# The six products of a panel step ordered by token half instead of by product

## The reference

```python
qa, ka, va, qb, kb, vb, gates = split_proj(rmsnorm(xp, g_norm1[l]), w_in[l])
oa = swa_prompt(qa, ka, va, rel_bias_table, swa_sinks[l])     # sliding-window attention
ob = sb_prompt(qb, kb, vb)                                    # stick-breaking attention
xp = merge_ffn(xp, oa, ob, gates, w_proj_a[l], w_proj_b[l], w_out[l], g_norm2[l], w_up[l], w_down[l])
...
def merge_ffn(x, oa, ob, gates, w_proj_a, w_proj_b, w_out, g_norm2, w_up, w_down):
    g = jax.nn.sigmoid(gates.astype(jnp.float32)).astype(x.dtype)
    merged = g[..., :D_MODEL] * (oa @ w_proj_a) + g[..., D_MODEL:] * (ob @ w_proj_b)
    x = x + merged @ w_out
    u = jnp.square(jax.nn.relu(rmsnorm(x, g_norm2) @ w_up))
    return x + u @ w_down
```

## Time and profile before

| | |
|---|---|
| Time, median of 3 runs | 832.81 us (832.44 to 832.97) |
| Profiled execution, its own time | 832.35 us |
| Its span in the profile | 830.5 us |
| PE busy | 818.9 us, 99% of the span, 6205 matmuls |
| PEld busy | 802.6 us, 97% of the span, 6205 weight loads |
| DVE, ACT, POOL busy | 624.1, 391.5, 294.9 us |
| Granted TensorE clock | 0.998 of full speed |
| DMA | 78.18 MB, mean 94 GB/s |

### The profile page before, as it was taken

How to read it: one execution, slowest core, us unless ns; L and a number is a source line. 1 busy time by engine, 2 the same in 40 slices (tenths; PEclk the granted TensorE clock), 3 DMA queues, 4 the chain that set the end, 5 groups by cost and what they waited for, 6 DMA issues and landing times.

```text
span 830.5 us, 16017 instructions
## 1 busy us (share of the span) xinstructions
PE 818.9 (99%) x6205; PEld 802.6 (97%) x6205; DVE 624.1 (75%) x1075; ACT 391.5 (47%) x668; POOL 294.9 (36%) x213
## 2 busy tenths in 40 slices
PE   9999999999999999999999999999999999999996
PEld 7999999999999989999999999999999999999995
DVE  5587876356889999876338888488965889488996
ACT  5657775244667757653332333233433243333532
POOL 2562222225545544254444200642025400552330
PEclk9999999999999999999999999999999999999999
DMA  8743112451112211143313113422134213422203
GB/s 279 257 148 100 52 51 65 152 166 52 52 52 82 70 51 51 51 165 127 102 53 102 52 52 102 152 70 83 51 101 128 74 51 101 132 70 66 85 2 115
DMA packets 68449, 78.18 MB, mean 94 GB/s; under 512 B 2552, under 2 KB 65072, under 8 KB 68016
## 3 DMA queue, kind: packets, MB, share of 16 engines
q1 hardware_dynamic: 68080, 76.92, 28.8%
q10 hardware_dynamic: 320, 0.60, 0.2%
HBM read 70.15 MB, written 8.93 MB: 95 GB/s over the span
## 4 chain that ended last, share of the span: by engine, by line
PE 87%; DVE 9%; issue 2%; ACT 1%; DMA 1%; ACTq 0%; DVEq 0%
PE pan L1567 56%; PE pan L1783 12%; PE att L1783 11%; PE att L1721 1%; PE att L1694 1%; PE pan L1623 1%; DVE sp_lo L1161 1%; PE att L1711 1%; PE att L1567 1%; DVE sp_hi L1159 1%; DVE xT L1400 1%; PE att L1863 1%; DMA grow<-in_g 1%; PE pan L1656 1%; DVE ob_lo L1223 1%
## 5 line engine op out<-in xcount | busy, mean ns | idle before, releaser
L475 POOL TENSOR_TENSOR w_lo<-raw,w_hi 128x512 fp32r<-128x512 f32 x160 | 222.0, 1413 | 422.0 <-ACT w_hi L817 180.0
L1567 PE MATMUL pan<-a_hi,w_hi 128*128 128x288 f32 x624 | 133.7, 295 | 0.0
L1567 PE MATMUL pan<-a_lo,w_hi 128*128 128x288 f32 x624 | 133.4, 295 | 0.0
L1567 PE MATMUL pan<-a_hi,w_lo 128*128 128x288 f32 x624 | 132.9, 295 | 0.0
L1567 PE MATMUL pan<-h_hi,w_hi 128*128 128x288 f32 x512 | 109.6, 295 | 0.0
L1567 PE MATMUL pan<-h_lo,w_hi 128*128 128x288 f32 x512 | 109.4, 295 | 0.0
L1567 PE MATMUL pan<-h_hi,w_lo 128*128 128x288 f32 x512 | 109.0, 295 | 0.0
L1567 PEld LDWEIGHTS pan<-a_hi,w_hi 128*128 128x128 f32 x624 | 99.7, 188 | 1.0
L1567 PEld LDWEIGHTS pan<-a_hi,w_lo 128*128 128x128 f32 x624 | 100.0, 188 | 0.0
L1567 PEld LDWEIGHTS pan<-a_lo,w_hi 128*128 128x128 f32 x624 | 99.5, 188 | 0.0
L1783 PE MATMUL pan<-F_hi,w_hi 128*128 128x288 f32 x320 | 95.7, 299 | 0.6 <-DVE xT L1400 0.6
(11 more groups left out here) (283 smaller groups left out, 1766.8 us busy)
## 6 DMA issues: line engine op xcount, KB each, us to landing
raw<-in_w_in SPq DMA_DIRECT2D x34, 512.0 KB, 4.9
raw<-in_w_up SPq DMA_DIRECT2D x32, 512.0 KB, 4.8
raw<-in_w_down SPq DMA_DIRECT2D x32, 512.0 KB, 4.8
raw<-in_w_out SPq DMA_DIRECT2D x8, 512.0 KB, 4.1
x_spill<-xT SPq DMA_DIRECT2D x1, 2304.0 KB, 7.0
xT<-x_spill SPq DMA_DIRECT2D x1, 2304.0 KB, 11.0
x_rows<-in_x_prompt SPq DMA_DIRECT2D x4, 512.0 KB, 6.7
raw<-in_w_pa SPq DMA_DIRECT2D x4, 512.0 KB, 4.6
```

Source lines behind the costliest of these rows:

```text
L475: last = nc.gpsimd.tensor_tensor(w_lo[:, slot, k:k + 4, :], raw[:, rs, k:k + 4, j * P:(j + 1) * P], w_hi[:, slot, k:k + 4, :].bitcast(F32) ...
L1567: got = nc.tensor.matmul(out[:, h, 0:HALF], w, x[:, h * HALF:(h + 1) * HALF], start=first and n == 0, stop=last and n == 2)
```

## The change

In `mm3` the two loops are exchanged. Before, each of the three products is issued for the first half of tokens and then for the second. Now the three products of the first half come first, then the three of the second. Flags (`start` with the first product, `stop` with the last) stay with their product, so each PSUM bank still gets its three terms in the same order. No offset of a buffer, no wait and no other engine's instruction is touched.

```diff
             def mm3(out, wh, wl, xh, xl, first, last):
 
-                for n, (w, x) in enumerate(((wh, xh), (wh, xl), (wl, xh))):
-                    for h in range(2):
+                for h in range(2):
+                    for n, (w, x) in enumerate(((wh, xh), (wh, xl), (wl, xh))):
                         got = nc.tensor.matmul(out[:, h, 0:HALF], w, x[:, h * HALF:(h + 1) * HALF],
                                                start=first and n == 0, stop=last and n == 2)
                 return got
```

## The result

The change makes the kernel slower by a quarter of a per cent: 834.94 us at the median of 17 runs against 832.81 us at the median of 17 of before, a ratio of 1.0023 with a 95% interval of 1.0016 to 1.0030. One run after the change, 992.03 us at a granted clock of 0.752, counts in the median and not in the ratio; without it the median is 834.82 us. The forecast was 838.2 us, in a range of 829.4 to 841.5: the direction was right and the time inside the range, but of the 5.4 us of loss that were forecast only 2.1 came.

The account below looks back on a forecast made before the run. The prediction took TensorE's distance between matmul starts as the bound: 3,840 panel matmuls moving to 133.3 ns add 5.4 us, everything else 0, so 832.8 + 5.4 = 838.2 us, in a range of 829.4 to 841.5 us.

Parts of the forecast that it names:

- What bounds the kernel: TensorE, busy 818.9 of 830.5 us: time is its number of matmuls times the distance between their starts.
- So one bank three times in a row has no price of its own: Panels: three successive matmuls to one PSUM bank cost nothing, since products do that and reach 131.1 ns.
- I take the high rung as the panels' new one: +5.4 us: All 3,840 panel matmuls go to 133.3 ns between starts, 512.0 us against 506.6; chance 0.42.
- the middle one: Distance of 132.2 ns between matmul starts, 793.3 ns per six; seen in panels in the old order.
- the low rung: Distance of 131.1 ns between matmul starts, 786.7 ns per six; seen in panels and products before the change.
- A change between high and low parts moves the read address by 32 bytes against a grid of 64: Panel steps: such changes take the time; the new order has two from high to low and two back, before one each.
- The direction: Sign of the whole change: slower with chance 0.59, same 0.19, faster 0.22.
- The ladder: Six matmuls of a step take 786.7, 793.3 or 800 ns, 6.7 ns apart; any other time would disprove the reason.
- The rival "by turns": Panels take both of the products' distances, 131.1 and 133.3 ns, by turns: +1.1 us (-0.3 to +2.5); chance 0.25.
- The dearer rung: Panels: both changes from high to low cost the dear one's time, 135.0 ns: +8.7 to +11.8 us; chance 0.14.
- All on the low rung: All panel matmuls at 131.1 ns: -3.1 us, with the first chunk's products -3.7 us; chance 0.19.
- The products' own shift: Down projection's products may take another distance from the phase the panels leave: 0 taken, -0.6 to +1.2 us allowed.

Follow-up runs that it names:

- e3: Changed kernel with the output bank alternating from matmul to matmul, reads in the new order; 834.41 us, ratio 1.0024 to the kernel before.
- e16: Kernel before (old order) with high parts of `a` and `h` at residue 64, low parts at 32 modulo 256; 834.85 us, ratio 1.0020.
- e1: Changed kernel (new order) with the activations' low parts at the same residue as the high parts, 64 modulo 256; 833.53 us, ratio 1.0014 to before.
- e2: Kernel before (old order) with the activations' low parts at the same residue as the high parts; 833.88 us, ratio 1.0013.
- e13: Changed kernel (new order) with low parts of `a` and `h` at residue 32 modulo 256, high parts kept at 64; 830.58 us, ratio 0.9974 to before.
- The snake: Third order at present offsets: first half high, low; second half low, high; then low weights with second half, first half; 835.11 us, ratio 1.0030 to before.
- e8: The kernel before, run again without any change; 832.18 us.
- e12: Changed kernel (new order) with high parts at residue 0 and low parts at 32 modulo 256; 835.50 us, ratio 1.0036 to before.
- e17: e13 with `ob_lo` and the products' `F_hi` and `F_lo` at residues 64 and 32 too, new order; 829.74 us, ratio 0.9952 to before.
- e9: New order with `a` and `h` at residues high 0, low 224 modulo 256, and `a` moved 256 bytes later; 833.53 us, ratio 1.0010 to before.
- e10: New order with `a` and `h` at residues high 0, low 224, and the second area holding `h` 256 bytes later; 833.66 us, ratio 1.0011 to before.

## Why the prediction was right in direction and wrong in size

**What bounds the kernel: right.** The loss is in the distance between starts of panel matmuls (0.56 ns x 3,840 = 2.15 us, against 2.13 us between the medians), and nothing is left over for another place. Waits stayed, loads stayed at 6205, and the groups' busy time rose to 151 us as computed.

**"So one bank three times in a row has no price of its own": right,** and shown by e3, where the banks alternate and the times stay.

**"I take the high rung as the panels' new one: +5.4 us": the step that failed.** It rested on "no panel is on the high rung in the old order and no product on the middle one, so the rungs on offer seem to go with the order". They go with the pair of order and addresses. The two were never seen apart in the trace of before, since each order had its own residues. e16 has the old order on the high rung, and the changed kernel itself has the new order on the middle one. The term of the sum that was mis-sized is thus the panels' new rung: put at 133.3 ns for all 3,840, it measured 132.2 and 133.0 ns by stretches, 132.49 on average, and +2.15 us in place of +5.4. The caution in the same paragraph, that the products' addresses aren't the panels', was the true point, and it should have cost the high rung its lead: with it gone, the products said nothing on the panels beyond a spread of 131 to 133.3 ns. I used it against the low rung alone.

**"A change between high and low parts moves the read address by 32 bytes against a grid of 64": half right.** The shift is needed for the order to matter at the present place of the high part: without it e1 and e2 are alike at 132.2 ns. The grid of 64 was an assumption that no row showed, and residues modulo 64 don't name the rungs: e13 has the same ones as the changed kernel and another distance. But counting the changes doesn't give the price. The snake with two a step has 132.8 ns, dearer than the 132.49 ns on average of the new order with four, and the new order at 64 and 32 has all four and the lowest rung of all.

**The direction: in part luck.** At 64 and 32, with as many changes by 32 bytes as at 64 and 96, the same exchange of loops gains 3.8 us (e13, e16). No reason in the prediction tells these two cases apart, so it couldn't have known the sign for this kernel's offsets.

**The ladder: incomplete.** I took the distances as the step's 786.7, 793.3 or 800 ns. A pattern may repeat over several steps, and it is its whole length that falls on the ladder: in the changed kernel 2,393.3 ns for three steps (359 x 6.67), in the snake 1,593.3 ns for two (239 x 6.67). So 133.0 and 132.8 ns are rungs too. The prediction had called its reason wrong if a step took a time off its ladder, and the single steps of 799 and 801 ns do. The step of 6.7 ns held; the row of six matmuls to which I applied it did not.

**The rival "by turns"** had a price of -0.3 to +2.5 us, into which the 2.1 us fall, but for another pair of rungs than it named. What it had right is that stretches draw among rungs, which e8 shows. **The dearer rung** fell at these addresses: 133.0 ns was the dearest, though e12 shows that offsets can bring more. **All on the low rung** was off for this change and came true one edit further, in e17, with a price near the one given (-3.1 us there; -4.0 us in e17, 0.0048 x 832.81). Of that the panels have only 2.5 us, by their mean of 131.27 ns; the products have most of the rest.

**The products' own shift:** -0.6 to +1.2 us was allowed. The first chunk's went down to 131.1 ns and the second's up to 133.3, for a sum of about zero. e8 shows that such shifts come without any change.

**The rule of the Trainium skill** ("TensorE: Matmul & The Clock Gate", back-to-back issue gap), 122.5 ns whatever the order: the runs don't agree. The section calls this gap that of an isolated matmul and gives none for 288 columns with a weight load for each. The lowest distance of a long stretch in 18 kernels was 131.1 ns, and order and addresses moved it to 133.3.

**Open.** Why a given pair of order and residues has its rungs isn't explained; the traces show starts, not reads. Nor is it settled what makes one stretch draw 131.1 and another 133.3 at an entry. Residues modulo 512 (e9, e10) don't, and repeats of one kernel (e8) differ only in some places. The weights were never moved, so whether the residue against the weights counts or the address by itself is open too.

## What to carry to other kernels

Where TensorE runs without a gap and reads several operand tiles in turn, as here, take the order of the matmuls and the start addresses of the tiles as one parameter: an order that is tried at offsets chosen for another order is tested at those offsets alone. Read the distance from long pieces of the chain, stretch by stretch, since a mean over the kernel mixes rungs; and when a change of order loses a few tenths of a per cent, run it again with the low part on the other side of the high part before dropping it. Here that turned a loss of 0.23% into a gain of 0.26%, and of 0.48% with `ob` and the products' tiles moved too. What it does to other shapes no run here shows.

## What the runs showed of the hardware that I had not expected

- In these kernels a row of 288-column fp32r matmuls, each with its own weight load, locks onto a pattern whose length is a whole multiple of 6.67 ns, over one, two or three steps of six matmuls: 786.7, 793.3 and 800 ns a step, 1,593.3 for two, 2,393.3 for three. At the granted 2.4 GHz, 6.67 ns are 16 clocks. What repeats every 16 clocks is not shown.
- The low part 32 bytes below the high one modulo 256 bytes, in place of 32 above, is worth up to 1.9 ns per matmul (new order: 133.0 ns at 64 and 96, 131.1 at 64 and 32 in like stretches), and some 4 us of the kernel lie between two orders of the same six matmuls at the same offsets (e13, e16).
- In the new order it made no difference where in PSUM the results went: with banks alternating or not, three pieces of 384 took 50.77, 51.06 and 50.77 us in both kernels.
- One program's stretches draw different rungs in different executions (4.80 and 4.72 us for the same 36 products in two executions of the kernel before), so some of the spread between executions lies in TensorE's distance and in no wait.
